# Scan stage: the convolved rows return to token order by VectorE block transposes and transfers, and ScalarE makes the decay exponents

## What is computed

```
xbc = silu(depthwise_conv4(xbc) + conv_b)            # xs (4096) | B | C (8 groups x 128 each)
a_cs = cumsum(dt * a)                                # in two chunks of 128 tokens
y = (C B^T * exp(min(a_cs[l] - a_cs[s], 0)) * causal) @ (xs * dt)    # per head, inside a chunk
  + C @ state * exp(a_cs)  + ssm_d * xs              # state comes from the first chunk
y = rms_norm_per_group(y * silu(z)) * ssm_norm_w
```

## Time and profile before

| | us |
|---|---|
| time before, median of 3 runs (2071.75 to 2071.89) | 2071.82 |
| the profiled execution, its own time | 2071.25 |
| its span | 2069.6 |
| TensorE busy in the span | 2050.0 |
| VectorE busy | 1352.3 |
| ScalarE busy | 972.7 |
| GpSimd busy | 168.6 |

### The profile page before, as it was taken

How to read it: one execution, slowest core, us unless ns; L and a number is a source line. 1 busy time by engine, 2 the same in 40 slices (tenths; PEclk the granted TensorE clock), 3 DMA queues, 4 the chain that set the end, 5 groups by cost and what they waited for, 6 DMA issues and landing times.

```text
span 2069.6 us, 27656 instructions
## 1 busy us (share of the span) xinstructions
PE 2050.0 (99%) x9586; PEld 1703.5 (82%) x9586; DVE 1352.3 (65%) x1783; ACT 972.7 (47%) x1261; POOL 168.6 (8%) x263
## 2 busy tenths in 40 slices
PE   8999999999999999999999999999999999999997
PEld 7788888888888888888888888888888888888886
DVE  6755667666664578886678876766546646655664
ACT  5443545454543455554455544544434434444443
POOL 3000000000000011111011110110000000100000
PEclk9999999999999999999999999999999999999999
DMA  8656464545466656666656567676666666666663
GB/s 268 215 160 199 133 182 141 165 141 167 143 205 198 176 175 186 181 182 201 186 171 183 183 211 255 217 217 215 215 195 213 213 194 194 223 202 180 227 213 134
DMA packets 197145, 396.19 MB, mean 191 GB/s; under 512 B 13408, under 2 KB 13504, under 8 KB 195632
## 3 DMA queue, kind: packets, MB, share of 16 engines
q1 hardware_dynamic: 188656, 364.42, 57.1%
q0 software_dynamic: 8208, 29.75, 4.7%
q10 hardware_dynamic: 176, 0.53, 0.1%
HBM read 379.91 MB, written 2.16 MB: 185 GB/s over the span
## 4 chain that ended last, share of the span: by engine, by line
PE 94%; DVE 2%; issue 2%; ACT 1%; DVEq 0%; DMA 0%; POOLq 0%; POOL 0%; ACTq 0%
PE acc L294 29%; PE acc L296 29%; PE acc L295 29%; PE x L918 1%; PE tr L329 1%; DVE lo L261 1%; PE x L854 1%; PE tr L876 1%; DMA raw<-w_proj_ssm 0%; PE x L861 0%; PE tr L878 0%; PE tr L869 0%; PE tr L881 0%; PE x L930 0%; PE x L329 0%
## 5 line engine op out<-in xcount | busy, mean ns | idle before, releaser
L261 DVE TENSOR_TENSOR lo<-raw,hi 128x1024 fp32r<-128x1024 f32 x688 | 839.3, 1233 | 490.0 <-ACT hi L255 481.1
L255 ACT ACTIVATE hi<-raw 128x1024 fp32r<-128x1024 f32 x688 | 718.6, 1058 | 655.4 <-PE acc L296 610.3
L294 PE MATMUL acc<-hi,LAh 128*128 128x512 f32 x1848 | 734.8, 398 | 1.2 <-DVE lo L261 1.2
L296 PE MATMUL acc<-hi,LAl 128*128 128x512 f32 x1848 | 721.4, 390 | 0.0
L295 PE MATMUL acc<-lo,LAh 128*128 128x512 f32 x1848 | 720.6, 390 | 0.0
L294 PEld LDWEIGHTS acc<-hi,LAh 128*128 128x128 f32 x1848 | 347.3, 188 | 74.0 <-issue 3.6
L296 PEld LDWEIGHTS acc<-hi,LAl 128*128 128x128 f32 x1848 | 347.0, 188 | 72.9
L295 PEld LDWEIGHTS acc<-lo,LAh 128*128 128x128 f32 x1848 | 347.4, 188 | 71.7 <-issue 1.7
L294 PE MATMUL acc<-hi,LBh 128*128 128x512 f32 x896 | 350.1, 391 | 0.7 <-DVE lo L261 0.7
L296 PE MATMUL acc<-hi,LBl 128*128 128x512 f32 x896 | 349.0, 389 | 0.0
L295 PE MATMUL acc<-lo,LBh 128*128 128x512 f32 x896 | 348.9, 389 | 0.0
(11 more groups left out here) (304 smaller groups left out, 1210.6 us busy)
## 6 DMA issues: line engine op xcount, KB each, us to landing
raw<-w_in SPq DMA_DIRECT2D x304, 512.0 KB, 3.8
raw<-w_up SPq DMA_DIRECT2D x128, 512.0 KB, 4.0
raw<-w_down SPq DMA_DIRECT2D x128, 512.0 KB, 4.7
raw<-w_proj_ssm SPq DMA_DIRECT2D x64, 512.0 KB, 4.6
raw<-w_proj_nsa SPq DMA_DIRECT2D x32, 512.0 KB, 4.4
raw<-w_out SPq DMA_DIRECT2D x32, 512.0 KB, 5.1
W<-acs_rows POOLq DMA_DIRECT2D x8, 1024.0 KB, 5.0
W<-TB POOLq DMA_DIRECT2D x48, 128.0 KB, 4.2
```

The costliest lines, as they stand in the source:

```text
L255: act.activation(hi[:, sl, :, :], raw[:, sl, :, :], ACT.Copy).then_inc(s_hi, 1)
L261: dve.tensor_tensor(lo[:, sl, :, :], raw[:, sl, :, :], hi[:, sl, :, :].bitcast(F32), ALU.subtract).then_inc(s_lo, 1)
L294: pe.matmul(o, xh, wh, start=(k == 0), stop=False)
L296: x = pe.matmul(o, xl, wh, start=False, stop=(k == KT - 1))
```

## The change

- TensorE: `turn_back` and its eight transposes are gone, with the events that it used (`E_L1`, `E_L2` and `E_PB2` count one event per group now, not two).
- VectorE: `turn_rows` in slot 13, ahead of `scan_split`: a drain and two block transposes of XC into TB. `scan_exponents` is gone from slots 1 and 2. `scan_inputs` moves from slot 15 to slot 1 of the next iteration.
- GpSimd: `spread_rows`, four transfers from TB back into XC's tile, named XS, behind `rms` and ahead of `stage_scan`. `skip_term` moves to the start of the next iteration.
- ScalarE: `token_rows` moves from slot 15 to slot 1 of the next iteration and copies from XS in SBUF; `scan_exp` begins with eight Relus of 128x128 (scale -1, bias the column sum) and a drain, then Exp with scale -1. It moves from slots 2 and 3 to slots 1 and 2.
- The loops of ScalarE, VectorE and GpSimd over the groups are written out. The temporary tile PT of the projection between them is XDT, not XC.

```diff
-E_L1 = E_X0 + 2
-E_L2 = E_L1 + 8
-E_PB2 = E_L2 + 6
+E_L1 = E_X0 + 1
+E_L2 = E_L1 + 4
+E_PB2 = E_L2 + 3
...
-        PT = XC.rearrange("p a s -> p (a s)").rearrange("p (t n) -> p t n", t=2)
+        PT = XDT
+        XS = XC.rearrange("p a s -> p (a s)")
...
+            def spread_rows(t):
+
+                pool.wait_ge(s_xb, t + 1)
+                for a in range(4):
+                    pool.dma_start(XS[:, S * a:S * (a + 1)], TB[32 * a:32 * (a + 1), :].rearrange("i (b n) -> i b n", b=4)).then_inc(s_xsp, 16)
...
-            def scan_iteration(t, m, e):
+            def scan_iteration(t, m):
+                if t:
+                    skip_term(t - 1)
                 stage_conv(m, 4 * t)
                 load_rows(t)
-                if not (isinstance(t, int) and t == 0):
+                if t:
                     rms(2 + 2 * t, NC, RS[:, 0:2])
+                spread_rows(t)
                 stage_scan(t)
-                skip_term(t, e + 1)
...
-            def turn_back(e, m):
-
-                pe_event(pe, e, [(s_xs, m + 2)])
-                for t in range(2):
-                    for ct in range(4):
-                        x = pe.transpose(TR[t][:, ct * P:(ct + 1) * P], XC[:, ct, t * P:(t + 1) * P], identf[:, :])
-                    x.then_inc(s_tr, 1)
-
-            def scan_iteration(C, par, e, m, g=None):
+            def scan_iteration(C, par, e, g=None):
                 hooks = scan_hooks(g) if g is not None else {}
                 hooks[8] = hooks.get(8, []) + [lambda: pe_turn(pe, e, XR, [(s_acc, C + 1)])]
-                hooks[15] = [lambda: turn_back(e + 1, m)]
...
-            def token_rows(e):
+            def token_rows(g):
+                act.wait_ge(s_xsp, 64 * g + 64)
+                v = XS.rearrange("p (a t c i) -> p t c a i", a=4, t=2, c=4)
                 for t in range(2):
-                    act.wait_ge(s_tr, 2 * e + t + 1)
-                    act.activation(XTOK[:, t, :], TR[t][:, :], ACT.Copy).then_inc(s_tra, 1)
+                    x = act.activation(XTOK[:, t, :].rearrange("p (c a i) -> p c a i", c=4, a=4), v[:, t, :, :, :], ACT.Copy)
+                x.then_inc(s_xt, 1)
 
             def scan_exp(g, c):
-                act.wait_ge(s_pl, 2 * g + c + 1)
-                act.activation(W[:, :, c, :], W[:, :, c, :], ACT.Exp).then_inc(s_dx, 1)
+                act.wait_ge(s_na, g + 1)
+                act.wait_ge(s_row, 16 * g + 16)
+                for h in range(8):
+                    act.activation(W[:, h, c, :], W[:, h, c, :], ACT.Relu, bias=NAs[:, c, h:h + 1], scale=-1.0)
+                act.drain()
+                act.activation(W[:, :, c, :], W[:, :, c, :], ACT.Exp, scale=-1.0).then_inc(s_dx, 1)
...
-                return {2: [lambda: scan_exp(g, 0)], 3: [lambda: scan_exp(g, 1), lambda: scan_state(g)], 9: [lambda: scan_squares(g)],
+                return {1: [lambda: token_rows(g), lambda: scan_exp(g, 0)], 2: [lambda: scan_exp(g, 1)], 3: [lambda: scan_state(g)], 9: [lambda: scan_squares(g)],
...
-                hk[15] = [lambda: take_z(C + 1, (par + 1) % 2, m), lambda: token_rows(e + 1)]
+                hk[15] = [lambda: take_z(C + 1, (par + 1) % 2, m)]
...
-            def scan_exponents(g, c):
-                dve.wait_ge(s_na, g + 1)
-                dve.wait_ge(s_row, 16 * g + 16)
-                for h in range(8):
-                    x = dve.tensor_scalar(W[:, h, c, :], W[:, h, c, :], NAs[:, c, h:h + 1], 0.0, ALU.subtract, ALU.min)
-                x.then_inc(s_pl, 1)
-
...
-                return {0: [lambda: scan_first(g)], 1: [lambda: scan_exponents(g, 0)], 2: [lambda: scan_exponents(g, 1)],
+                return {0: [lambda: scan_first(g)], 1: [lambda: scan_inputs(g)],
                         3: [lambda: scan_w(g, 0)], 4: [lambda: scan_w(g, 1)], 5: [lambda: scan_y0(g)], 8: [lambda: scan_y1(g)],
...
+            def turn_rows(m):
+                dve.drain()
+                for h in range(2):
+                    x = dve.transpose(TB[:, :].rearrange("p (b t c i) -> p c t b i", b=4, t=2, c=4)[:, 2 * h:2 * h + 2, :, :, :],
+                                      XC[:, 2 * h:2 * h + 2, :].rearrange("p c (t j b) -> p c t b j", t=2, b=4))
+                x.then_inc(s_xb, 1)
...
+                hk[13] = [lambda: turn_rows(m)] + hk.get(13, [])
+                hk[15] = [lambda: take(C + 1, (par + 1) % 2, ZR[:, 1, :], xa + 2)]
```

More of the change, by code:

```diff
@@ L199, in build @@
         s_pg = sem("scan_operands_staged")
+        s_xb = sem("conv_blocks_turned")
+        s_xsp = sem("conv_blocks_spread")
+        s_xt = sem("token_rows_copied")
         s_xd = sem("scan_inputs_ready")
@@ L207, in build @@
         s_row = sem("cumulative_rows_spread")
-        s_pl = sem("decay_exponents_ready")
         s_na = sem("column_sums_staged")
@@ L702, in _ @@
             pool.wait_ge(s_ato, 16)
-            def scan_iteration(t, m, e):
+            def scan_iteration(t, m):
+                if t:
+                    skip_term(t - 1)
                 stage_conv(m, 4 * t)
                 load_rows(t)
-                if not (isinstance(t, int) and t == 0):
+                if t:
                     rms(2 + 2 * t, NC, RS[:, 0:2])
+                spread_rows(t)
                 stage_scan(t)
-                skip_term(t, e + 1)
[L712 to L716, removed]
+            for t in range(8):
+                scan_iteration(t, 4 + t)
+            skip_term(7)
             rms(18, NC, RS[:, 0:2])
@@ L961, in _ @@
             for i in range(0, 3):
-                scan_iteration(C_L2 + 2 * i, C_L2 % 2, E_L2 + 2 * i, 9 + i, i + 4)
+                scan_iteration(C_L2 + 2 * i, C_L2 % 2, E_L2 + i, i + 4)
             hooks = last_hooks(scan_hooks(7))
@@ L1206, in scan_iteration @@
                 hk[12] = hk.get(12, []) + [lambda: conv_tanh(m)]
-                hk[15] = [lambda: take_z(C + 1, (par + 1) % 2, m), lambda: token_rows(e + 1)]
+                hk[15] = [lambda: take_z(C + 1, (par + 1) % 2, m)]
                 slots(act, split_hi, C, 16, hk)
             scan_iteration(C_X0, C_X0 % 2, E_X0, 4)
-            with act.Fori(0, 4) as i:
-                scan_iteration(C_L1 + 2 * i, C_L1 % 2, E_L1 + 2 * i, 5 + i, i, 4 * i)
+            for i in range(4):
+                scan_iteration(C_L1 + 2 * i, C_L1 % 2, E_L1 + i, 5 + i, i, 4 * i)
             with act.Fori(0, 2) as i:
                 slots(act, split_hi, C_PB1 + 2 * i, 16, {})
-            with act.Fori(0, 3) as i:
-                scan_iteration(C_L2 + 2 * i, C_L2 % 2, E_L2 + 2 * i, 9 + i, i + 4, 4 * i)
+            for i in range(3):
+                scan_iteration(C_L2 + 2 * i, C_L2 % 2, E_L2 + i, 9 + i, i + 4, 4 * i)
             hk = last_hooks(scan_hooks(7, 12))
@@ L1599, in scan_hooks, with scan_inputs, scan_iteration @@
             def scan_hooks(g, k0):
-                return {0: [lambda: scan_first(g)], 1: [lambda: scan_exponents(g, 0)], 2: [lambda: scan_exponents(g, 1)],
+                return {0: [lambda: scan_first(g)], 1: [lambda: scan_inputs(g)],
                         3: [lambda: scan_w(g, 0)], 4: [lambda: scan_w(g, 1)], 5: [lambda: scan_y0(g)], 8: [lambda: scan_y1(g)],
                         13: [lambda: scan_split(g, k0)]}
-            def scan_inputs(t, e):
-                dve.wait_ge(s_tra, 2 * e + 2)
+            def scan_inputs(g):
+                dve.wait_ge(s_xt, g + 1)
                 for c in range(2):
-                    x = dve.tensor_tensor(heads8(XDT[:, c, :]), heads8(XTOK[:, c, :]),
-                                          DT[:, c, ds(8 * t, 8)].unsqueeze(2).broadcast_to([P, 8, SH]), ALU.mult)
-                x.then_inc(s_trd, 1)
+                    dve.tensor_tensor(heads8(XDT[:, c, :]), heads8(XTOK[:, c, :]),
+                                      DT[:, c, 8 * g:8 * g + 8].unsqueeze(2).broadcast_to([P, 8, SH]), ALU.mult)
                 dve.drain()
                 dve.tensor_tensor(heads8(XDS[:, :]), heads8(XDT[:, 0, :]),
-                                  DST[:, ds(8 * t, 8)].unsqueeze(2).broadcast_to([P, 8, SH]), ALU.mult).then_inc(s_xd, 1)
-            def scan_iteration(C, par, e, m, xa, t, g=None, k0=None):
+                                  DST[:, 8 * g:8 * g + 8].unsqueeze(2).broadcast_to([P, 8, SH]), ALU.mult).then_inc(s_xd, 1)
+            def turn_rows(m):
[4 more added lines that the diff above has]
+                x.then_inc(s_xb, 1)
+            def scan_iteration(C, par, m, xa, g=None, k0=None):
                 hk = scan_hooks(g, k0) if g is not None else {}
@@ L1621, in scan_iteration @@
                 hk[12] = [lambda: conv_out(m, XC[:, :, :])]
-                hk[15] = [lambda: take(C + 1, (par + 1) % 2, ZR[:, 1, :], xa + 2), lambda: scan_inputs(t, e + 1)]
+                hk[13] = [lambda: turn_rows(m)] + hk.get(13, [])
+                hk[15] = [lambda: take(C + 1, (par + 1) % 2, ZR[:, 1, :], xa + 2)]
                 slots(dve, split_lo, C, 16, hk)
@@ L1632, in add_gated @@
```

(10 more changed lines are left out.)

10 lines of the change are left out of this document (5 added, 5 removed).

## The result

The changed kernel takes **2077.11 us** (median of 8 runs, 2075.24 to 2078.95). The kernel before took 2071.60 beside it (8 runs, 2070.78 to 2071.89). The ratio is 1.0026, with an interval of 1.0016 to 1.0035: slower by 5.5 us, where 6.2 were forecast. The profiled execution has a span of 2075.6 against 2069.6 us, so the trace has 6.0 us to explain.

What follows compares the result with a forecast made beforehand. TensorE, busy 99% of the span, was taken to bound the kernel. Stalls of 13.7 us less 7.0 for the removed transposes gave +6.7 on 2071.8, stated as 2078 us, range 2069 to 2085.

Steps and rivals of the forecast that it cites:

- `turn_back`: TensorE's eight transposes per group: one costs 0.88 us, all on the path, so removing eight saves 7.0 us.
- The chain that then ends last: From VectorE's transposes through ScalarE's tanh, token rows, Relus and Exps to `scan_w`: `scan_y0` can start at Z+18.99.
- Z: Start of the last TensorE hook of an iteration, 1074.48 us in the one shown; moments are Z plus microseconds.
- The stall of 1.15 us from the chain: TensorE's wait before `scan_y0` in each group that follows another at once, if the spread rows are there in time.
- the transfers: GpSimd's four spreading transfers, priced from later stages at mean 7.94 us after the transposes: 0.57 us more stall per usual group.
- if the transfers land within 6 us: One of the signs named in advance that would show the prediction wrong.
- Groups 0 and 1: Stalls before `scan_y0` of 2.4 us and 3.3 us, late rows in both; 0.6 of the latter already present.
- Group 4: Follows four chunks without hooks; chain ends near Z+16.5, before TensorE arrives at Z+17.84, so no stall.
- The rest is near zero: loops written out: Loops written out save register work of under 0.1 us here and there, off the path.
- Spread early and chain shorter: Rival: prompt transfers and a Relu step of 0.25 leave the time within 0.2%, 2073 us; chance 0.24.
- Whole gain kept: Rival: Relu step of 0.22 or less and prompt rows, no usual group stalls, faster, 2066 us; chance 0.16.
- Late transfers: Rival: transfers land at 9.2 us, or GpSimd and instruction loading add a microsecond; stalls 3 us, 2087.5 at most; chance 0.12.

Runs made afterwards that it cites:

- run 1: Changed kernel with ScalarE's second decay step, `scan_exp(g, 1)`, moved from slot 2 to slot 3 behind `scan_state`: 2071.01 us.
- run 4: Changed kernel with four Relus of 128x256 per chunk in place of eight of 128x128, odd heads' exponents not the reference's: 2069.25 us.
- run 9: Changed kernel without GpSimd's four transfers per group, so the token rows are not the reference's: 2072.96 us.
- run 2: On top of run 1, VectorE's multiply by the tanh moved from slot 0 to slot 2, behind `scan_inputs`: 2067.42 us.
- run 10: Run 2 with the four spreading transfers issued by ScalarE in slot 14 instead of by GpSimd: 2072.82 us.
- run 5: Kernel before with only the exponents moved, made by ScalarE in slots 1 and 2, TensorE's transposes kept: 2070.74 us.
- run 7: Kernel before with only two of the eight transposes of `turn_back` run, other token rows not formed: 2067.41 us.
- run 8: Kernel before with only the loops over the groups written out on GpSimd, ScalarE and VectorE: 2073.10 us.
- run 3: Changed kernel with only VectorE's multiply by the tanh moved from slot 0 to slot 2, behind `scan_inputs`: 2079.89 us.
- run 6: Changed kernel with exponents made by VectorE again in slots 1 and 2, ScalarE's Exps in slots 2 and 3, return path kept: 2085.68 us.

## Why the prediction was right, and where it was not

**The mechanism was right.** "The chain that then ends last" was VectorE's transposes, z's half, the tanh, the token rows, both decay steps, `scan_w`; the chain in the trace has just these, and its end is 0.08 to 0.09 us from the sum (Z+18.76 for `scan_w` against 18.84, Z+18.90 for `scan_y0` against 18.99). Runs 1 and 4 each shorten it on ScalarE alone and take the waits away; run 9 leaves it as it is and the waits stay in six of seven groups. `turn_back` was right too: where nothing waits (run 2) usual `scan_y0`s are 51.25 to 51.33 us apart, 0.88 to 0.96 less than the 52.21 before.

**The stall of 1.15 us from the chain came out, with help.** The distance from one usual `scan_y0` to the next grew by 0.25 us (1.26 over five); with the 0.88 of `turn_back` that is an effective stall of 1.13. It lies at `scan_y0` and `scan_state`, when the 0.16 that each bracket leaves out is counted. But by run 9 only 0.85 of it is there without the transfers; the other 0.28 is the chain's later start behind GpSimd's norm, which the forecast did not have.

**The term that was mis-sized: the transfers.** "Averaging what each of the 16 exceeds 7.40 by gives 0.57 us" took the four transfers' price from other stages. Here they landed in 2.7 us from issue, not in the 4.2 of those, and outside group 0 ScalarE did not wait for them once: 0 in place of 0.57, in five usual groups 2.9 us. The prediction's own sign for this, "if the transfers land within 6 us", was met, by the 5.8 worked out above. What the transfers did cost there is the 0.28 by way of the norm. The estimate from the Trainium skill ("DMA: Bandwidth & Descriptors", section "Anatomy of one DMA"), about 2.3 us, was the nearer one in the usual group, and the rows that I set against it were of another stage; group 0 with 4.1 us fits those. The DMA engines were busy for 82% of the 7 us from the first issue in group 0 and for 79% in the usual group, so their load hardly tells the two apart; why group 0's took longer stays open.

**Groups 0 and 1.** `scan_y0` of group 0 started at Z+19.51, so its stall was 1.67 us (Z+17.84 is where TensorE would arrive) against 2.4; ScalarE did wait for the rows, as forecast, but they came 7.31 us after the transposes and not 7.94. In group 1 the stall was 2.71 (Z+20.55) against 3.3, and the reason given for it failed: no wait for rows stands there. The tanh came at Z+5.10 and the token rows at Z+7.96, so it was VectorE's late slot 13 through z's half, a path that the forecast had only as the 0.6 already present. (Z of group 1 before was 777.78, not 777.94; the present wait was then 0.77 with its overlap, and the two slips cancel.)

**Group 4** had no stall, as forecast, but the piece shows -0.17 and not -0.88. Most of the difference is one gap of TensorE put down to issue, 0.42 and the overlap of 0.16, which the trace of before does not have:

```profile
940.21 0.47 PE L296 MATMUL acc<-hi,LBh 128*128 128x512 f32 x1 [0.42 <-issue]
```

It is in every profile without `turn_back` (0.41 to 0.48, in run 10 0.18) and in none of the four with it (before, runs 5, 7 and 8), run 8's unrolled loops among them. So it goes with the transposes gone from that place, not with the loops; by what means stays open. "The rest is near zero: loops written out" had no row for its 0.1 us, and run 8 measured 1.4 us for the loops alone, which just reaches no change.

**What made the total come out.** Less in the usual groups (-2.9) and in groups 0 and 1 (-0.75 each), more from the clock (+1.6), GpSimd's norm at the turn of `y` (+1.05), group 4 (+0.7) and the stage before the scan (+0.5). That the forecast of 2078 came so close is in part luck: 4.4 us too much and 3.8 too little cancelled.

**The rivals.** *Spread early and chain shorter*: half of it held, prompt transfers, but not the shorter Relu. *Whole gain kept* named the right point, the length of ScalarE's chain: run 4 brings the Relus to 0.21 us per head and lands at 2069.25, not at the 2066 of this rival, with the waits at `scan_state` and at the turn of `y` still there. *Late transfers* did not happen.

**The version that wins** keeps both halves of the change and moves two steps that were not urgent behind the urgent one: 2067.42 us, 4.3 below the kernel before. By runs 1 and 3, the second decay step sets `scan_y0`, and moving the multiply helps only once that is away (-3.6 us on top of run 1, of which some 1.6 may be run 1's clock at 72 us; +2.8 alone). The cost was thus the order of work on two queues, not the work's amount.

## What to carry to other kernels

When work is taken off the engine that bounds a kernel and put in front of another engine's queue, sum the whole chain to the next wait of the first engine, and then ask which links in that queue are not yet needed: moving those behind can be worth more than the change itself. Two waits in series are one: removing the earlier one moves it to the later, and only the chain's own length counts. A price for a transfer should come from its own stage, and one for a VectorE step from a row with the same neighbour on GpSimd.

## What the runs showed of the hardware that was not expected

- VectorE's eight `tensor_scalar` of 128x128 fp32 took 3.28 us beside a GpSimd `tensor_tensor` of 128x512 and 1.65 us with GpSimd idle (run 6).
- GpSimd's small steps became slower in iterations in which it had issued four transfers itself: 0.60 instead of 0.26 us of gap in the usual groups, and 1.64 instead of 0.72 for one step at the end. Both went back when the transfers were left out (run 9) or issued by ScalarE (run 10), but for one gap in each, of 0.56 and 0.77.
- TensorE's granted clock fell to 0.50 for some 3 us behind waits of 1.54 us (changed kernel), of 1.36 and 0.98 us (run 3), of 0.94 (run 6) and of 1.77 (run 1), but not behind one of 1.68 (changed kernel) nor behind those of 0.96 and 1.65 us (run 3). At about 1.6 us each, such a drop costs more than the wait of a usual group. The length of the wait does not tell them apart; what does stays open.
- Four 128 KB transfers between SBUF tiles landed 2.7 us after issue in one stage and 4.1 to 4.2 in others.
